# A two-block transformer of four layers: layers written out without a barrier, and attention scores from one 128-row tile

## The reference

```python
q = (_rmsnorm(c_q, q_norm) @ w_uq).reshape(B, S, H, 64 + 32)
q_nope, q_rot = q[..., :64], _rope(q[..., 64:], cos, sin)
k_nope, v = split(_rmsnorm(c_kv, kv_norm) @ w_ukv)        # 64 and 64 columns a head
k_rot = _rope(k_rope_raw, cos, sin)                        # 32 columns, one for all heads
s = (einsum(q_nope, k_nope) + einsum(q_rot, k_rot)) * 96 ** -0.5
_rope(t) = concat(t1 * cos - t2 * sin, t1 * sin + t2 * cos)
```

## Time and profile before

| what | value |
|---|---|
| median of 3 executions | 3039.44 us (3038.32 to 3043.8) |
| the profiled execution, its own time | 3038.53 us |
| its span, first to last instruction | 3036.6 us |
| PE matmul busy | 2760.3 us (91%) |
| DVE / ACT / POOL busy | 1575.6 / 1290.2 / 476.9 us |
| DMA | 445.06 MB, mean 147 GB/s |
| mean granted TensorE clock | 0.951 |

### The profile page before, as it was taken

How to read it: one execution, slowest core, us unless ns; L and a number is a source line. 1 busy time by engine, 2 the same in 40 slices (tenths; PEclk the granted TensorE clock), 3 DMA queues, 4 the chain that set the end, 5 groups by cost and what they waited for, 6 DMA issues and landing times.

```text
span 3036.6 us, 51797 instructions
## 1 busy us (share of the span) xinstructions
PE 2760.3 (91%) x21412; PEld 2543.6 (84%) x21412; DVE 1575.6 (52%) x2182; ACT 1290.2 (42%) x1830; POOL 476.9 (16%) x199
## 2 busy tenths in 40 slices
PE   7989899798989989888889898998988888989898
PEld 7988799798879979877779788988987777888898
DVE  5566555556655555532545515555553264451555
ACT  3435444343544434434523454444444452444443
POOL 0000000000000000033424650000003352465000
PEclk9999999899999989998999999999999899999999
DMA  8754465575546556622322544655662231244564
GB/s 231 211 155 153 125 185 178 166 211 153 153 132 183 177 153 185 183 90 79 102 64 73 172 139 147 185 166 168 186 181 78 83 110 59 85 160 132 159 185 126
DMA packets 622824, 445.06 MB, mean 147 GB/s; under 512 B 27904, under 2 KB 589344, under 8 KB 622176
## 3 DMA queue, kind: packets, MB, share of 16 engines
q1 hardware_dynamic: 622688, 443.09, 49.0%
HBM read 441.99 MB, written 1.05 MB: 146 GB/s over the span
## 4 chain that ended last, share of the span: by engine, by line
PE 85%; DVE 9%; ACT 3%; issue 2%; DMA 0%; POOL 0%; SPq 0%; DVEq 0%; ACTq 0%; POOLq 0%
PE ps L360 18%; PE ps L361 18%; PE ps L362 18%; PE ps L376 7%; PE ps L377 6%; PE ps L378 6%; PE ps L586 2%; PE ps L610 1%; PE ps L403 1%; PE ps L1370 1%; ACT w_hi L627 1%; PE ps L1177 1%; PE ps L1084 1%; PE ps L1360 1%; DVE zT L1512 1%
## 5 line engine op out<-in xcount | busy, mean ns | idle before, releaser
L360 PE MATMUL ps<-in_hi,w_hi 128*128 128x256 f32 x4352 | 1261.6, 290 | 64.1 <-POOL w_lo L821 31.0
L361 PE MATMUL ps<-in_lo,w_hi 128*128 128x256 f32 x4352 | 1247.3, 287 | 0.0
L362 PE MATMUL ps<-in_hi,w_lo 128*128 128x256 f32 x4352 | 1246.5, 286 | 0.0
L627 ACT ACTIVATE w_hi<-raw 128x1024 fp32r<-128x1024 f32 x788 | 832.1, 1057 | 938.3 <-PE ps L362 624.1
L821 DVE TENSOR_TENSOR w_lo<-raw,w_hi 128x1024 fp32r<-128x1024 f32 x594 | 727.6, 1225 | 738.4 <-ACT w_hi L627 737.5
L360 PEld LDWEIGHTS ps<-in_hi,w_hi 128*128 128x128 f32 x4352 | 852.1, 196 | 86.2 <-issue 34.2
L361 PEld LDWEIGHTS ps<-in_lo,w_hi 128*128 128x128 f32 x4352 | 852.1, 196 | 7.0 <-issue 0.5
L362 PEld LDWEIGHTS ps<-in_hi,w_lo 128*128 128x128 f32 x4352 | 850.9, 196 | 0.0
L821 POOL TENSOR_TENSOR w_lo<-raw,w_hi 128x1024 fp32r<-128x1024 f32 x194 | 476.4, 2463 | 2310.8 <-ACT w_hi L627 2309.9
L376 PE MATMUL ps<-w_hi,hid_hi 128*128 128x512 f32 x704 | 276.0, 392 | 0.0
L377 PE MATMUL ps<-w_lo,hid_hi 128*128 128x512 f32 x704 | 275.9, 392 | 0.0
(11 more groups left out here) (301 smaller groups left out, 2691.7 us busy)
## 6 DMA issues: line engine op xcount, KB each, us to landing
raw<-in_w_ffn_in SPq DMA_DIRECT2D x176, 512.0 KB, 3.7
raw<-in_w_mix SPq DMA_DIRECT2D x112, 512.0 KB, 3.6
raw<-in_ffn_w_gate SPq DMA_DIRECT2D x88, 512.0 KB, 3.9
raw<-in_ffn_w_up SPq DMA_DIRECT2D x88, 512.0 KB, 3.8
raw<-in_ffn_w_down SPq DMA_DIRECT2D x88, 512.0 KB, 3.6
raw<-in_w_ffn_out SPq DMA_DIRECT2D x88, 512.0 KB, 3.5
raw<-in_w_in SPq DMA_DIRECT2D x40, 512.0 KB, 3.7
raw<-in_w_out SPq DMA_DIRECT2D x32, 512.0 KB, 3.5
```

The source lines that it names most:

```text
L360: nc.tensor.matmul(o, lh, rh, start=first, stop=False, **kw)
L361: nc.tensor.matmul(o, lh, rl, start=False, stop=False, **kw)
L362: return nc.tensor.matmul(o, ll, rh, start=False, stop=last, **kw)
L627: nc.scalar.activation(w_hi[:, e % SPLIT, :], raw[:, e % RAW, :], ACT.Copy).then_inc(sem("split_high"), 1)
```

## The change

1. *Layers written out.* Loops over layers become Python loops; pieces, norms, turns and rows are counted on through all four layers (`enter1`, `enter2` set the bases), so the semaphores of feed-forwards and turns join `WHOLE` and are never cleared. `sp_first`, `act_first`, `low_first` and their semaphores go: the next layer's first pieces are ordinary pieces.
2. *No barrier at a layer's end.* The remaining semaphores are still cleared once a layer, but engines report (`layer_done`) before the layer's second feed-forward, SP clears in the midst of it (`layer_clear`, behind tile 6), and the wait stands at the next layer's head (`layer_begin`).
3. *Constant products at each turn.* `pe_warm(n)` issues n fp32 matmuls of `ones` by `ones`, 128x256, into PSUM bank 5, which nothing reads: 15 after each stage of the first block, 14 in the second, and 8 more at the head of its layers.
4. *Latent heads in one 128-row tile.* The columns of `w_uq` are ordered so that one output tile holds a head's 64 plain, 32 rotary and 32 swapped rows (for odd heads the plain rows last). A constant tile `turns` holds 1, cos and sin on those rows, and DVE forms a head group's queries with one product from PSUM. The keys hold `k_rope` twice beside the head's 64 rows, and a head's scores are one matmul over 128 rows for each token half.
5. *Loads at the start.* x and identity come ahead of the pieces, the other constants at tile 2; the first three pieces are split in the order 0, 1, 2 (before: 1, 2, 0).

```diff
+        def pe_warm(pe, n):
+            for _ in range(n):
+                nc.tensor.matmul(ps[:, WARM_BANK, 0:S], ones[:, 0:P], ones[:, :], start=True, stop=True)
...
-            for t in (4, 5, 6, 7, 0, 1, 2, 3):
+            for t in range(MLA_HEADS):
                 for k in range(2):
-                    mm = nc.tensor.matmul(ps[:, (0, 1, 4, 5)[t // 2], (t % 2) * S:(t % 2 + 1) * S], w_uq[:, k, t * P:(t + 1) * P],
+                    mm = nc.tensor.matmul(ps[:, (4, 5, 0, 1)[t // 2], (t % 2) * S:(t % 2 + 1) * S], w_uq[:, k, t * P:(t + 1) * P],
                                           c_q[:, k, :], start=(k == 0), stop=(k == 1))
...
-            pe.wait_ge(sem("mla_taken"), 1)
+            pe.wait_ge(sem("mla_q_set"), 1)
...
-            pe.wait_ge(sem("mla_taken"), 4)
-            pe.wait_ge(sem("mla_rope"), 2)
+            pe.wait_ge(sem("mla_taken"), 5)
+            pe.wait_ge(sem("mla_q_set"), 2)
             def scores(h, t):
-                o, r = 64 * (h % 2), ROPE * (h % 4)
-                return [(mla_qn[o:o + 64, h // 2, t * P:(t + 1) * P], mla_kn[o:o + 64, h // 2, :]),
-                        (mla_qr[r:r + ROPE, h // 4, t * P:(t + 1) * P], k_rope[r:r + ROPE, 0, :])]
+                return [(mla_q[h % 2][:, h // 2, t * P:(t + 1) * P], mla_k[h % 2][:, h // 2, :])]
...
-            nc.scalar.activation(mla_qr[:, :, :], bank2(4), ACT.Copy).then_inc(sem("mla_taken"), 1)
-            nc.scalar.activation(mla_qn[:, :, :], bank2(0), ACT.Copy).then_inc(sem("mla_taken"), 1)
-            act.wait_ge(sem("mla_kv_ready"), 1)
-            nc.scalar.activation(mla_kn[:, :, :], bank2(6), ACT.Copy).then_inc(sem("mla_taken"), 1)
+            act.wait_ge(sem("mla_rope"), 1)
+            rows = slice(0, 64), slice(64, P)
+            for odd in range(2):
+                at = rows[1 - odd]
+                turned_k = k_rope[at, 0:1, :].broadcast_to([64, 4, S])
+                nc.scalar.activation(mla_k[odd][at, :, :], turned_k, ACT.Copy).then_inc(sem("mla_taken"), 1)
+            act.wait_ge(sem("mla_k_ready"), 1)
+            for odd in range(2):
+                at = rows[odd]
+                nc.scalar.activation(mla_k[odd][at, :, :], bank2(6, 64, 64 * odd), ACT.Copy).then_inc(sem("mla_taken"), 1)
...
+            for odd in range(2):
+                dve.wait_ge(sem("mla_q_ready"), odd + 1)
+                table = turns[odd][:, :].rearrange("p (o t) -> p o t", o=1).broadcast_to([P, 4, S])
+                nc.vector.tensor_tensor(mla_q[odd], bank2(4 - 4 * odd), table, ALU.mult).then_inc(sem("mla_q_set"), 1)
...
-        def layer_end(eng, n):
+        def layer_done(eng):
             eng.drain().then_inc(arrived, 1)
-            if eng is not nc.sync:
-                eng.wait_ge(cleared, n)
-                return
+        def layer_clear(sp, layer):
+            sp.wait_ge(arrived, 5 * (layer + 1))
+            sp.sem_inc(all_arrived, 1)
...
+        def layer_begin(eng, layer):
+            if layer:
+                eng.wait_ge(cleared, layer)
...
-            with pe.Fori(0, LAYERS) as l:
-                pe_turn(pe, 0, x_tok, BY_COLUMNS, waits=False)
+            for l in range(LAYERS):
+                enter1(l)
+                layer_begin(pe, l)
+                pe_turn(pe, 0, x_tok, BY_COLUMNS, waits=l > 0)
                 pe_ffn(pe, 0, E1_FFN1, C1_FFN1)
-                pe_turn(pe, 0, x_tok, BY_COLUMNS)
+                pe_warm(pe, 15)
+                pe_turn(pe, 1, x_tok, BY_COLUMNS)
...
-                pe_turn(pe, 1, x_tok, BY_COLUMNS)
+                pe_warm(pe, 15)
+                pe_turn(pe, 2, x_tok, BY_COLUMNS)
+                layer_done(pe)
                 pe_ffn(pe, 1, E1_FFN2, C1_FFN2)
-                layer_end(pe, l + 1)
-
-            with pe.Fori(0, LAYERS) as l:
+                pe_warm(pe, 15)
+
+            for l in range(LAYERS):
+                enter2(l)
+                layer_begin(pe, LAYERS + l)
+                pe_warm(pe, 8)
                 pe_turn(pe, 0, z_tok, BY_TOKENS)
                 pe_ffn(pe, 0, E_FFN1, C_FFN1)
+                pe_warm(pe, 14)
                 pe_turn(pe, 1, z_tok, BY_TOKENS)
...
+            for i, at in enumerate((64, 0)):
+                nc.vector.memset(turns[i][64 - at:P - at, :], 1.0)
+                nc.vector.tensor_copy(turns[i][at:at + ROPE, :], cos[at:at + ROPE, :])
+                nc.vector.tensor_copy(turns[i][at + ROPE:at + 2 * ROPE, :], sin[at + ROPE:at + 2 * ROPE, :])
```

More of the change, by code:

```diff
@@ L190, in build @@
         pos_i = sb("pos_i", [P, S], I32)
+        turns = [sb(f"turns{i}", [P, S]) for i in range(2)]
         arena = sb("arena", [P, 23184])
@@ L646, in act_turn @@
                 ins.then_inc(sem("in_high"), 1)
-        def last_use(before, e):
-            return before - (before - 1 - e) % SPLIT
-        def first_order(before):
-            return sorted(range(SPLIT), key=lambda e: last_use(before, e))
-        def act_first(act, layer, order, before=None, part=range(SPLIT)):
-            for i in part:
-                e = order[i]
-                act.wait_ge(FIRST_HERE[e], 16 + layer * 16)
-                if before is not None:
-                    act.wait_ge(sem("piece_used"), last_use(before, e))
-                nc.scalar.activation(w_hi[:, e, :], raw[:, e, :], ACT.Copy).then_inc(first_high, 1)
-        def act_layer(act, layer):
-            act.sem_inc(sem("split_high"), SPLIT)
-            act.wait_ge(first_rest_here, 16 * (RAW - SPLIT) + layer * (16 * (RAW - SPLIT)))
         def act_silu_table(act):
@@ L688, in after @@
                     act_sqrt_table(act)
[L689 removed]
+                elif e0 + e + SPLIT < E_LAST:
                     act_split(act, e0 + e + SPLIT, it)
[L691 to L692 removed]
             ffn_steps(act, after)
@@ L2137, in layer2 @@
                 sp_linear(sp, E_O, rows(wo[l]))
-                sp_ffn(sp, E_FFN2, *ffn2(l, 1),
-                       between=lambda t: t != 5 or across(post_gain[3], a["norm_post"][l, 3], "post_here3"))
-                if following is not None:
-                    sp_first(sp, *following, before=E_END)
-                layer_end(sp, l + 1 + LAYERS)
-            with sp.Fori(0, LAYERS - 1) as l:
-                layer2(l, ffn2(l + 1, 0))
-            layer2(LAYERS - 1)
+                if not last:
+                    layer_done(sp)
+                sp_ffn(sp, E_FFN2, *ffn2(l, 1), between=last_small)
+            for l in range(LAYERS):
+                layer2(l, l == LAYERS - 1)
+            sp.wait_ge(sem("x_ready"), HALF * (1 + 4 * LAYERS))
             sp.dma_start(out, x_tok[:, :, :]).then_inc(stored, 16)
```

327 lines of the change are left out of this document (171 added, 156 removed).

## The result

| | median, us | runs |
|---|---|---|
| before | 3041.62 (3038.32 to 3045.27) | 4 |
| changed kernel | 2999.27 (2997.47 to 3006.01) | 4 |
| forecast | 2992 (2980 to 3007) | |

The ratio is 0.9865, 95% interval 0.9851 to 0.9878: 1.35% faster. The time lies in the range, 7 us above the forecast. Between the profiled executions the span went from 3036.6 to 2996.4 us, 40.2 less, where the prediction's terms sum to 46.8.

The account below looks back on a forecast made before the run. TensorE's matmuls were taken as the bound, 2760 us of a 3036.6 us span. Terms 28 + 5.9 + 1.4 + 6.1 + 1.4 + 4 = 46.8 us off 3038.5 gave 2992 us, range 2980 to 3007.

Parts of the forecast that it names:

- latent scores: Second block's attention: two 128-row matmuls a head replace four of 64 and 32 rows, saving 28 us over 16 heads.
- first turn between layers: First block's layer boundary: without barrier and branch back, 12.44 us plus 0.7 for memsets instead of 19.05; saves 5.9 us.
- first to second kind: Turn between the blocks: ACT's work moves up, new cos and sin tables fit in DVE's idle time; saves 1.4 us.
- second kind's layers: Turn between the second block's layers: 7.1 us excess goes, except about 1.0 from late transposes; saves 6.1 us.
- start: Program start: splitting pieces in order 0, 1, 2 leaves one low part after the last landing; saves 1.0 us.
- constant products, other eight turns: Warm-up matmuls at the turns: a quarter of the 16 us upper end, so 4 us saved; lower end -6.
- rival A: The clock holds through the turns, so the warm-ups' whole 16 us come: 2980 us; chance 0.09.
- C: Latent tile pays half or less: 14 us less saved, 3006, or by the skill's rule 28 less, 3020; chance 0.08.
- E: Code fetch becomes the bound in PE's longer straight code: 18 stalls, 73 us, 3065; chance 0.03.
- D: A branch back's stall stays as a fetch in the long code: 4 us at two places, 3000; chance 0.05.
- B: Warm-ups stand in the way: each turn pays 0.5 to 1 us, term -6 instead of 4, 3002; chance 0.10.
- F: Waits on semaphores counted on from the layer before hold engines like the barrier; turns keep 12 us, 3004; chance 0.03.

Follow-up runs that it names:

- experiment 1: The changed kernel without a single constant product, nothing else different: 3000.7 us.
- experiment 6: The changed kernel with a head's latent scores again as four matmuls of 64 and 32 rows, the swapped rotary rows left out: 3030.63 us.
- experiment 7: The changed kernel with each latent head's two score matmuls over 128 rows issued twice: 3014.8 us.
- experiment 5: The changed kernel with the cos and sin tables built at program start and the first-block layer-head memsets moved behind dve_turn: 2992.57 us.
- experiment 8: The changed kernel with the barrier put back at the three layer boundaries, in straight code without a branch back: 2999.83 us.
- experiment 4: The changed kernel with its own constant products, plus only those between the transposes' halves and, in the second block, behind them: 2984.76 us.
- experiment 3: The changed kernel with constant products filling every whole turn, before, between and (second block) behind the transposes: 2986.25 us.
- experiment 11: The kernel of experiment 10 with constant products (21, 26, 26) meant for three long waits in the second block's mixing stage: 2992.75 us.
- experiment 2: The changed kernel itself run once more, unedited: 3001.26 us.
- experiment 10: The changed kernel with the edits of experiment 3 and experiment 5, plus constant products around the transposes at program start: 2979.92 us.

## Why the prediction was right, and where it was off

| term | forecast | measured |
|---|---|---|
| latent scores | 28 | 27.8 in the attention, 25.7 in the mixing stages |
| first turn between layers | 5.9 | 5.7, with the matmuls behind it 4.7 |
| first to second kind | 1.4 | 0.3, with the matmuls behind it 0.2 |
| second kind's layers | 6.1 | 6.0, with the matmuls behind it 6.9 |
| start | 1.0 | 1.2, with the matmuls behind it 0.0 |
| end | 0.4 | 0.5 |
| constant products, other eight turns | 4 | 1.9 with the matmuls behind them; against experiment 1 3.9 |

**Latent scores**: right in sum and in reason (two matmuls of 0.43 us each instead of the 2.50 us of four, and the price of the change of tile gone too, experiments 6 and 7). PE stayed busy through a head and no other engine became the bound. What the mixing stages lost again is 2.1 us, shared between places with a lower clock; no run isolates it.

**First turn between layers**: 13.33 us where 13.1 were expected. The memsets cost 0.9, not 0.7 (experiment 5), and only 0.1 of their 1.0 us was hidden. The term left out what the clock does behind the turn: 15 slow matmuls instead of 5, 1.0 us. The sum took barrier and branch back together here and named no share; 3.87 us of the loss were the branch back, as at the other boundary (experiment 8). The sum was not harmed, since both go.

**First to second kind**: the step "the new tables of cos and sin are six small DVE operations in the idle before" failed. DVE isn't idle there. They ran from 1067.21 to 1069.04, as the normalised x came, and held the reciprocal for 1.1 us; the barrier's gain of 1.4 went into them.

**Second kind's layers**: right, with the 2.2 us of lateness behind 22 products (experiment 4 prices it at 1.9) and no "issue".

**Start**: 1.24 us earlier, as forecast, and 26 slow matmuls instead of 13 took it back. A term at a stretch with a cold clock needs the matmuls behind it.

**Constant products**: the reason stood in the text (the clock "will often fall in the gap, with the slow stretch as long as before"), and so it went. Only the size, a quarter of 16, was a guess, and that it lies near is partly luck: it is 1.9 us in the eight turns against the kernel before, 3.9 against experiment 1, and 0 to 2 in the time. Most of rival A's 16 us were there, but not for products that stand ahead of the transposes alone: filled, the eleven turns with their matmuls are 14.3 us shorter than the changed kernel's (experiment 3), and the eight turns alone 10.3 us shorter than before. The 16 was somewhat high: the slow matmuls of before at all eleven turns, 5 to 21 at eight of them, are 117 at 0.09 us more, 10.9 us, and the rest of it was to come from the transposes.

**The total**: 40.2 us between the profiled spans where 46.8 were added up. By the stretches, the latent part with its mixing stages gave 2.3 us less than forecast, the three turns at the layers' heads together 1.6, the start 1.0, the products 2.1 and the end 0.1 more.

Of the rivals, none held. C and E are excluded by the heads and by the missing "issue" (0.6 us of PE's idle time in all), D likewise. B holds at the turn into the last layer alone, where the products cost 1.0 us, and the price was in the sum. F in its form (a turn that waits on "cleared") isn't seen.

## What to carry to other kernels

Where constant matmuls are to hold TensorE's clock, look at every idle stretch up to the next dense stage, not at the longest: here 15 products ahead of the transposes bought next to nothing, and a few more between and behind them 13 to 15 us. Then place each in the timeline directly at the wait that it fills, since before a ready piece it only delays (experiment 11). When barriers and loops go together, time the boundary a third way, with the barrier in straight code: three quarters of what looked like the barrier was the loop. And judge an edit of a few us by the length of its own turn and by several kernels, since the clock's slow stretches fell otherwise in nearly every kernel here, for some 5 us either way.

## What the runs showed of the hardware

- Two profiled executions of one kernel agree in their slow matmuls, within one, at ten turns of eleven (experiment 2); kernels that differ only in later code do not, and the times of this kernel's four executions spread over 8.5 us. The Trainium skill (TensorE: Matmul & The Clock Gate, What's actually happening) says that the number of slow matmuls varies from run to run of one kernel; here the executions agree at all turns but one, where it was 1 and then 14, so the trace agrees for that turn alone.
- PE's branch back over a long body: 3.87 and 4.03 us, once before the first matmul of the body and once after eleven transposes. In straight code of twice the length 0.6 us of PE's idle time in all ends in "issue".
- fp32 scores over 128 rows: 0.86 us for four records, 1.06 behind matmuls that use part of the array; in parts of 64 and 32 rows 2.50 us for eight, in full height 1.73, or 1.93 behind matmuls that use part of the array. Eight records of 64 rows in both halves of the array take 1.14 us, four in one half 1.13 (experiment 7).
- The linear attention's 48 score records of 64 columns (24 fp32 matmuls; the expectations count records) took 9.8 us from first to last start at a granted clock of 0.50 and 6.5 at 0.81, behind constant products (experiments 10 and 11). RWKV's four chunks took 95.9 us at a mean clock of 0.98 and 94.6 at 1.00: the clock was hardly down there, so there was little to gain.
